# Dividing by the softmax sums after the values product, and moving half of the transposed exponentials from PSUM on VectorE

## The reference, cut to what matters

```python
def gqa(q, k, v):
    ...
    s = jnp.einsum('bqkgd,bskd->bkgqs', qg, k, preferred_element_type=jnp.float32) * (HEAD_DIM ** -0.5)
    p = jax.nn.softmax(s, axis=-1).astype(v.dtype)
    o = jnp.einsum('bkgqs,bskd->bqkgd', p, v)
```

## Time and profile before

| | before |
|---|---|
| median of 3 runs | 1474.59 us (1474.55 to 1475.87) |
| the profiled execution | 1474.66 us |
| its span (first to last instruction) | 1472.9 us |
| TensorE busy | 1399.6 us, 95% |
| VectorE busy | 541.2 us, 37% |
| ScalarE busy | 402.4 us, 27% |
| attention, layer 0 | about 167 to 226 us of the span |
| attention, layer 1 | about 721 to 762 us |

### The profile page before, as it was taken

The page is one execution under the profiler, slowest core; times in us unless marked ns, Lnnn a source line. Parts: engine busy times, 40 slices in busy tenths (PEclk is TensorE's granted clock), DMA queues, the critical chain, the costliest instruction groups (busy, mean ns, idle before and its releaser), DMA issues.

```text
span 1472.9 us, 26027 instructions
## 1 busy us (share of the span) xinstructions
PE 1399.6 (95%) x11437; PEld 825.6 (56%) x11437; DVE 541.2 (37%) x980; ACT 402.4 (27%) x708; POOL 0.2 (0%) x4
## 2 busy tenths in 40 slices
PE   6899899999999999989888999999999999999896
PEld 3688657888888888878666334333333333333231
DVE  2799894522322323368874102111020201101022
ACT  3523385522222223366483101100101101000011
POOL 0000000000000000000000000000000000000000
PEclk9899899999999999999999999999999999999999
DMA  9997903532330143411408999999999999999995
GB/s 350 385 342 269 372 3 109 178 98 73 115 113 30 58 171 94 154 67 58 172 2 311 403 360 408 405 408 406 408 408 406 408 405 409 405 408 408 405 409 235
DMA packets 144952, 391.47 MB, mean 266 GB/s; under 512 B 7072, under 2 KB 38336, under 8 KB 144832
## 3 DMA queue, kind: packets, MB, share of 16 engines
q1 hardware_dynamic: 144000, 388.85, 69.4%
q10 hardware_dynamic: 832, 0.88, 0.2%
HBM read 388.66 MB, written 1.05 MB: 265 GB/s over the span
## 4 chain that ended last, share of the span: by engine, by line
PE 83%; DVE 6%; DMA 6%; SPq 2%; ACT 1%; issue 1%; DVEq 0%; ACTq 0%
PE bank L1200 25%; PE bank L1158 9%; PE bank L1008 5%; PE bank L1006 5%; PE bank L1007 5%; PE bank L729 4%; PE bank L730 4%; PE bank L731 4%; DMA weight_ring<-in_exp_w 3%; PE bank L1015 3%; PE bank L1017 3%; PE bank L1016 3%; PE bank L1166 3%; PE bank L675 2%; DMA weight_ring<-in_w_ada 2%; DVE weight_ring L1861 2%
## 5 line engine op out<-in xcount | busy, mean ns | idle before, releaser
L1200 PE MATMUL bank<-weight_ring,gathered 128*32 128x512 f32 (+1 forms) x3840 | 393.4, 561 | 7.5 <-issue 4.6
L1200 PEld LDWEIGHTS bank<-weight_ring,gathered 128*32 128x32 f32 x3840 | 123.1, 110 | 251.4 <-issue 250.9
L1158 PE MATMUL bank<-weight_ring,scratch 128*32 128x512 f32 x1344 | 157.2, 593 | 0.7 <-DMA weight_ring<-in_exp_w 0.7
L2206 DVE TENSOR_TENSOR scratch<-scratch,bank 64x512 f32<-64x512 f32 (+1 forms) x60 | 38.4, 639 | 260.0 <-ACT scratch L1663 257.9
L1008 PE MATMUL bank<-slot_halves,slot_halves 128*128 128x512 f32 x336 | 130.7, 389 | 0.0
L1007 PE MATMUL bank<-hT_halves,slot_halves 128*128 128x512 f32 x336 | 130.7, 389 | 0.0
L1006 PE MATMUL bank<-slot_halves 128*128 128x512 f32 x320 | 124.6, 389 | 0.0
L730 PE MATMUL bank<-hT_halves,slot_halves 128*128 128x512 f32 (+1 forms) x352 | 122.2, 347 | 0.0
L1861 DVE SCALAR_TENSOR_TENSOR weight_ring<-scratch,conv_weights,weight_ring 128x512 f32<-128x512 f32 (+1 forms) x207 | 121.3, 636 | 2.6 <-ACT weight_ring L1455 0.7
L729 PE MATMUL bank<-slot_halves,slot_halves 128*128 128x512 f32 (+1 forms) x284 | 106.0, 373 | 8.6 <-DVE slot_halves L1768 5.7
L1158 PEld LDWEIGHTS bank<-weight_ring,scratch 128*32 128x32 f32 x1344 | 42.5, 110 | 99.4 <-issue 97.1
(11 more groups left out here) (288 smaller groups left out, 1626.2 us busy)
## 6 DMA issues: line engine op xcount, KB each, us to landing
weight_ring<-in_exp_w SPq DMA_DIRECT2D x216, 1024.0 KB, 16.9
weight_ring<-in_w_ada SPq DMA_DIRECT2D x24, 2048.0 KB, 14.0
weight_ring<-in_exp_w SPq DMA_DIRECT2D x64, 768.0 KB, 15.1
weight_ring<-in_ffn_w SPq DMA_DIRECT2D x33, 1024.0 KB, 5.4
weight_ring<-in_w_in SPq DMA_DIRECT2D x8, 1024.0 KB, 11.5
weight_ring<-in_w_out SPq DMA_DIRECT2D x4, 2048.0 KB, 11.4
weight_ring<-in_w_in SPq DMA_DIRECT2D x2, 3072.0 KB, 15.2
hT<-in_x SPq DMA_DIRECT2D x1, 1024.0 KB, 6.0
```

The lines of the kernel that those rows point to most:

```text
L1158: i = mm(bank[6][quarter, :], at01[:, c0:c0 + BLOCK], w2[:, i_, half * 512:(half + 1) * 512], start=(first and i_ == 0), stop=(last and i_ ...
L1200: i = mm(ps[BLOCK * job:BLOCK * (job + 1), 0:cw], gathered_block(e, k, b), w[:, kk, a * cw:(a + 1) * cw], start=(k == 0), stop=(k == KT - 1))
```

## The change

Four things, in both layers:

1. The scaling (L1978, L1980) and `prob_ready` go. The transposes wait for the exponential itself (`exp_done`) and move bare exponentials.
2. Bank 4 (head 0) is copied by ScalarE as before; bank 5 (head 1) by VectorE. Each copy has a semaphore of its own, `pt_ready[0]` and `pt_ready[1]`.
3. For every two pairs VectorE takes the reciprocals of their four sums in one instruction (`sum_inv`). Behind the values of an odd pair TensorE issues four more products into the other half of bank 6: each spreads one column of reciprocals over 64 partitions.
4. ScalarE still copies the values from bank 6 to `hT`, but this now raises `o_raw`. VectorE then multiplies that tile by the spread reciprocals in bank 6, and this raises `o_ready`. The rounded copy on ScalarE comes one step later, so its loop has one step more.

```diff
@@ TensorE @@
                         for hh in range(2):
-                            pe.wait_ge(m["prob_ready"], 2 * p + hh + 1)
+                            pe.wait_ge(m["exp_done"], 2 * p + hh + 1)
...
-                                pe.wait_ge(m["pt_ready"], 2 * p + hh - 1)
+                                pe.wait_ge(pt_ready[hh], 16 * l + p)
...
-                        pe.wait_ge(m["pt_ready"], 2 * p + 2)
+                        for ready in pt_ready:
+                            pe.wait_ge(ready, 16 * l + p + 1)
                         if p % 2 == 0 and p:
                             pe.wait_ge(m["o_ready"], p // 2)
...
+                        if p % 2:
+                            pe.wait_ge(sum_inv, 8 * l + p // 2 + 1)
+                            for b in range(2):
+                                for hh in range(2):
+                                    u = 96 + 2 * (p - 1 + b) + hh
+                                    i = mm(bank[6][HD * hh:HD * hh + HD, S + b * P:S + (b + 1) * P],
+                                           att[:, u:u + 1].to_broadcast([P, HD]), ident, start=True, stop=True)
                         i.then_inc(m["pv_mm"], 1)
@@ ScalarE @@
-                for st in range(len(U) + 3):
+                for st in range(len(U) + 4):
                     p = st - 3
                     if 0 <= p < len(U) and p % 2 == 1:
                         c, _, _, sg = U[p]
                         act.wait_ge(m["pv_mm"], 16 * l + p + 1)
-                        f(hv[:, c, sg * S:(sg + 1) * S], bank[6][:, 0:S], ACT.Copy).then_inc(m["o_ready"], 1)
+                        f(hv[:, c, sg * S:(sg + 1) * S], bank[6][:, 0:S], ACT.Copy).then_inc(o_raw, 1)
+                    p = st - 4
+                    if 0 <= p < len(U) and p % 2 == 1:
+                        c, _, _, sg = U[p]
                         if l or sg:
                             act.wait_ge(m["o_ready"], p // 2 + 1)
                             f(mix_hi[l][c], hv[:, c, 0:TQ], ACT.Copy).then_inc(hx_hi, 1)
...
-                        for hh in range(2):
-                            act.wait_ge(m["pt_mm"], 2 * p + hh + 1)
-                            f(probT[2 * (p % 2) + hh][:, 0:n], bank[4 + hh][:, 0:n], ACT.Copy).then_inc(m["pt_ready"], 1)
+                        act.wait_ge(m["pt_mm"], 2 * p + 1)
+                        f(probT[2 * (p % 2)][:, 0:n], bank[4][:, 0:n], ACT.Copy).then_inc(pt_ready[0], 1)
@@ VectorE @@
+                def normalized(p):
+                    c, _, _, sg = U[p]
+                    dve.wait_ge(o_raw, 8 * l + p // 2 + 1)
+                    h = hv[:, c, sg * S:(sg + 1) * S]
+                    tt(h, h, bank[6][:, S:TT], ALU.mult).then_inc(m["o_ready"], 1)
...
+                    if st and st % 2 == 0:
+                        u = 2 * st - 4
+                        dve.wait_ge(m["exp_done"], 2 * st)
+                        dve.reciprocal(att[:, 96 + u:100 + u], att[:, 64 + u:68 + u]).then_inc(sum_inv, 1)
                     if st:
-                        n = TT - U[st - 1][2] * P
-                        for hh in range(2):
-                            u = 2 * (st - 1) + hh
-                            dve.wait_ge(m["exp_done"], u + 1)
-                            link(dve.reciprocal(att[:, 96 + u:97 + u], att[:, 64 + u:65 + u]))
-                            pr = prob[2 * ((st - 1) % 2) + hh][:, 0:n]
-                            ts(pr, pr, att[:, 96 + u:97 + u], None, ALU.mult).then_inc(m["prob_ready"], 1)
+                        p = st - 1
+                        n = TT - U[p][2] * P
+                        dve.wait_ge(m["pt_mm"], 2 * p + 2)
+                        if p >= 2:
+                            dve.wait_ge(m["pv_mm"], 16 * l + p - 1)
+                        dve.tensor_copy(probT[2 * (p % 2) + 1][:, 0:n], bank[5][:, 0:n]).then_inc(pt_ready[1], 1)
+                    if st >= 3 and st % 2 == 0:
+                        normalized(st - 3)
                 dve.wait_ge(m["root"], 3)
                 dve.reciprocal(rstd[0:TQ // 4, 0:P], rstd[0:TQ // 4, 0:P]).then_inc(norm_inv, 1)
+                normalized(len(U) - 1)
```

More of the change, by code:

```diff
@@ L266, in backbone @@
                  "glu",
-                 "conv_step", "exp_done", "prob_ready", "pt_mm", "pt_ready",
+                 "conv_step", "exp_done", "pt_mm",
                  "o_ready",
@@ L289, in backbone @@
             sem(n) for n in ["y_shift", "yt_ready", "scatter_mm", "scatter_added"])
+        sum_inv, o_raw = sem("sum_inv"), sem("o_raw")
+        pt_ready = [sem(f"pt_ready_{hh}") for hh in range(2)]
         slot_sel, slot_mm, slot_ready = (sem(n) for n in ["slot_sel", "slot_mm", "slot_ready"])
@@ L944, in _ @@
                                        start=(kt == 0), stop=(kt == nk - 1))
+                        if p % 2:
[5 more added lines that the diff above has]
+                                           att[:, u:u + 1].to_broadcast([P, HD]), ident, start=True, stop=True)
                         i.then_inc(m["pv_mm"], 1)
                 pe.wait_ge(m["exp_done"], 2 * len(U))
-                pe.wait_ge(m["pt_ready"], 2 * len(U))
+                for ready in pt_ready:
+                    pe.wait_ge(ready, 16 * l + len(U))
                 pe.wait_ge(m["o_ready"], len(U) // 2)
```

## The result

The changed kernel takes **1480.08 us**, median of 9 runs (1477.96 to 1481.67); the kernel before takes 1474.59, median of 9 (1471.90 to 1477.30). The ratio is 1.0038 [1.0030, 1.0046]: 5.5 us slower. The profiled execution of the changed kernel took 1481.67 us, with a span of 1479.9 (before: 1474.66 and 1472.9). It lies near the upper end of its runs and that of before in the middle of its own, so the two spans, 7.0 us apart, are not compared as a whole: I compare stages.

The account below looks back on a forecast made before the run. TensorE bounds the attention, with VectorE nearly level. Layer 0 +3.0 and layer 1 +1.1 make +4.1 us on the profiled 1474.66: 1478.8 us, chance 0.48, range 1473.5 to 1483.0.

Parts of the forecast that it names:

- The gate: Even steps from 4 on: values wait for VectorE's multiplication behind its copy; TensorE idle 1.19 us, bounds 0.9 and 1.5.
- the sums: Twelve groups of four spread products added to TensorE: 0.5 us a group, bounds 0.43 and 0.86.
- The start: Start of layer 0: without the scaling, transposes start at 173.27 and step 3 comes 0.9 us earlier.
- steps 3 to 7: Layer 0, 12.78 us before: two sums and two full gates make it 15.8, +3.0 us.
- steps 7 to 11: Layer 0, 12.86 us before: two sums and 0.4 us of mostly hidden gates, +1.4 us.
- step 11 to the end: Layer 0: −0.1 us to the last values, where VectorE paced before, and −0.4 behind the loop.
- layer 1: Attention of layer 1: step 3 comes 0.6 us earlier, later sums and gates cost +2.4, 0.7 given back; +1.1 us.
- Rival A: TensorE's granted clock falls in the new gaps once or twice, 1.7 to 3.4 us each: 1480.5 to 1483; chance 0.20.
- the signs for being wrong: Even pairs' values within 1.1 us of their transposes, other low-clock stretches than before, or another expert stage length.
- Rival B: The clock no longer falls at the start of layer 0: 2.6 us less, 1476.2; chance 0.17.
- Rival C: VectorE was the pacer nearly everywhere, so gate and sums are free and the relief counts: 1466.6; chance 0.10.
- The copy on the engine farther from PSUM: 24 copies moved to VectorE: 0.08 us more each, 1.9 us if all were exposed; not counted in the forecast.

Follow-up runs that it names:

- run 3: Changed kernel without the spread products for all odd pairs but the first of each layer (10 of 12 groups left out); 1476.28 us, ratio 1.0014.
- run 5: Run 2 without any division: no reciprocals, spread products or multiplication; 1464.64 us, ratio 0.9942.
- run 8: Run 2 with two transposes of reciprocals that VectorE writes 64 times each, in place of four spread products; 1471.80 us, ratio 0.9979.
- run 9: Run 8 with the copy of bank 5 on VectorE again, behind the multiplication; 1472.58 us, ratio 0.9990.
- run 1: Changed kernel with VectorE's multiplication of the output (even steps) moved ahead of its copy of bank 5; 1475.26 us, ratio 1.0000.
- run 2: Changed kernel with both copies back on ScalarE, the division still behind the values product; 1474.21 us, ratio 0.9998.
- run 4: Kernel before, scaling kept, with the twelve groups of spread products added and read by nobody; 1479.78 us, ratio 1.0034.
- run 6: Kernel before with 48 unread products of two columns added ahead of the program's projections; 1494.48 us, one execution.
- run 7: Run 2 with 48 unread products of two columns added ahead of the program's projections; 1487.26 us, one execution.

## Why the prediction was right, point by point

It said 1478.8 us, slower; the runs gave 1480.1. The gate, the sums and the place of the loss are as forecast. That the total came so close is in part luck: misses in the two layers cancel, and a pause of 1.3 us was not in the sum.

**The start, −0.9.** Scores of step 3 start 13.35 us behind the first scores, for 14.60: −1.25. The transposes start at 173.28, as said (173.27).

**The sums, 0.5 us a group.** 0.53 by their own start times, but a step grows by 0.44 (3.54 us for 3.10), which is the cheap bound, 0.43. The values' shape was the right row to price it from; the gap that I added to it was not there.

**The gate, 1.19 us.** The profile shows 1.20 of idleness, in both wide steps of layer 0 and in the last pairs of layer 1. The forecast was of another distance, from the transposes' start to the values, and that grew from 1.02 to 2.30 us, by 1.28. The chain adds to 2.30 where I had 2.21: copy 1.13 behind the transposes' start (said 1.15), multiplication 0.61 behind the copy (0.60), values 0.56 behind that (0.47), of which 0.15 is the way back to TensorE (said 0.05). Gate and sums together are 1.72 us in two steps, for 1.69: two small misses that cancel. A wait for the empty pipe (Trainium skill, VectorE: DVE Perf Modes, The DRAIN you can't avoid), read as the copy's full recorded length, would have put the multiplication at 0.69; the trace shows 0.61. The same section says that a next operation which is not held starts earlier, and the trace fits that.

**The sum.** The parts of layer 0:

| us | forecast | measured |
|---|---|---|
| start | −0.9 | −1.25 |
| steps 3 to 7 | +3.0 | +3.07 (180.93 to 196.78, before 12.78) |
| steps 7 to 11 | +1.4 | +1.42 (196.78 to 211.06, before 12.86) |
| step 11 to the end | −0.5 | −0.85 (211.06 to 228.48, before 18.27) |
| layer 0 | +3.0 | +2.39 |
| layer 1 | +1.1 | +1.68 |

In layer 1 the stretch from step 6 to the end of the values took +2.45 (said +2.4), but VectorE's relief ahead of step 3 was worth 0.13 and not 0.6: from 734.30 to 740.98 TensorE works through that stretch at the low clock without idle time, so it is not VectorE that is late there. The misses of the two layers cancel, 4.1 for 4.1, and that is luck. TensorE resumes after layer 0 at 228.48; I had said near 229.0:

```profile
225.71 1.09 PE L944 MATMUL bank<-weight_ring,scratch 128*64 128x128 f32 x16 [0.93 <-DVE hT L1964]
226.61 0.64 PE L953 MATMUL bank<-constants,softmax_stats 128*64 128x128 f32 x8
228.48 1.74 PE L677 MATMUL bank<-weight_ring,silu_c 128*32 128x128 f32 x56 [1.24 <-DVE hT L1964]
```

**What was missed: 1.3 us behind the attention.** The sum priced the added instructions by their run time alone. 96 more TensorE instructions, 64 of them ahead of this place, brought a pause of 1.29 us into an unchanged group, and 4.1 + 1.3 = 5.4 is the 5.5 of the medians. The runs show that the place of the pause goes with the count of TensorE's instructions ahead of it: in the modulation there is none in the kernel before nor in runs 3, 5, 8 and 9, which have 8, none, 16 and 16 more ahead, and there is one in the changed kernel and runs 1, 2 and 4, with 64 more, in run 6, with 96, and in run 7, with 160. The packets of the instruction queue, which start 2.4 to 2.7 us ahead of the end of each pause, speak for a fetch of instructions, without showing it. The number of packets on the pages does not: it is 94 in the changed kernel, but 93 in the kernel before and in every other variant, with the pause or without.

**Rival A, the clock falls in the new gaps: no.** Windows of the changed kernel, around the two gates of 1.20 us and around the widest gate of the context half (length, busy us of each engine, granted clock, DMA):

```profile
186.62:195.75 9.13, 6.73 (x65) 4.52 (x65) 6.53 (x14) 6.78 (x16) 0.00 (x0) 1.00 0.00 0
...
214.58:230.00 15.42, 11.05 (x185) 8.55 (x188) 11.46 (x29) 13.58 (x33) 0.00 (x0) 1.00 0.01 3
```

The granted clock stayed at 2.4 GHz, with TensorE busy 74% and 72% of the stretch. The rule that the engine's power follows its use (Trainium skill, Perfetto Trace Analysis, Matmul Optimizations) made a fall likely; no gap of 1.2 to 1.8 us brought one here (the longest, 1.78, is in step 4 of layer 1). Of the signs for being wrong one was met by the letter, a low stretch that before does not have, 3.4 us near 696. It lies ahead of layer 1's attention, in work that is unchanged, and the profiles of runs 1, 3, 7 and 9 have one there too. The other two were not met: the values of even pairs follow their transposes after 2.30 us, and the expert stage has the same length within 0.3 us.

**Rival B, the clock holds at the start: by execution.** Not in the changed kernel's profile, but in those of runs 3 and 5 (11.00 for 13.35), worth 2.35 us where I had 2.6.

**Rival C, VectorE sets the pace: partly.** Run 3 shows it: of the sums' 4.4 to 5.3 us only 2.5 came back when they were left out, the rest was hidden in waits. It was in the forecast for steps 11 and up and for early layer 1.

**The copy on the engine farther from PSUM.** It took 0.69 us for ScalarE's 0.59, which fits that the Trainium skill places ScalarE closer to PSUM (VectorE: DVE Perf Modes, Specifications). 24 x 0.10 is at most 2.4 us; moving them back won 5.9, and run 1, which changes the place in the list alone, won 4.8 of it. The place decided more than the length.

## What to carry to other kernels

When an operation moves to another engine, look at what stands behind it on that engine's list and who waits for that: here a copy that must wait for this step's transposes was put ahead of a multiplication that was ready, and changing their order won back 4.8 of 5.5 us. A division moved behind a product is free only if the engine that bounds the kernel gets little for it. Price what it gets from one step's start to the next and not by its own stretch: four thin products lengthen a step by 0.44 us, two full transposes of the same numbers by 0.36, while their own start times say 0.53 and 0.36. And compare stages from fixed marks in the timelines, since one pause or one stretch of low clock at an unchanged place is as large as the effect.

## What the runs showed of the hardware that I had not expected

- TensorE can pause 1.03 to 2.94 us at a place that goes with how many instructions it has run before. The timeline names no releaser. In all nine cases in these traces a packet of the instruction queue starts 2.43 to 2.73 us before TensorE goes on. It was 1.29 us of the changed kernel's loss, and in run 3 the 2.21 us in the expert stage cost nothing.
- In run 6, 96 passes of two columns with 128x128 weights took 20.62 us, 0.215 us each, at the low clock all through; the 16 before them in the same execution took 3.58 at that clock (0.224 each), and in the kernel before 1.95 at the full clock (0.122). Work of that size is not small beside an idle time of 5.7 us.
- Whether the granted clock falls at the start of layer 0 differed between executions with the same instructions up to there, and was worth 2.35 us. Over the runs of one kernel the time goes roughly with the mean granted clock: of the first variant 1472.03 us at 0.982 and 1482.05 at 0.973.
